# Two-layer transformer kernel: the rotary part of the latent attention scores from rounded values and their rests

## What is computed

```python
q = (rmsnorm_2(cq, q_norm_g) @ w_uq).reshape(B, S, MLA_HEADS, MLA_NOPE + MLA_ROPE)
q = jnp.concatenate([q[..., :MLA_NOPE], rope(q[..., MLA_NOPE:], pos)], axis=-1)
kv = (rmsnorm_2(ckv, kv_norm_g) @ w_ukv).reshape(B, S, MLA_HEADS, MLA_NOPE + MLA_V)
k_nope, v = kv[..., :MLA_NOPE], kv[..., MLA_NOPE:]
k_rope = rope(k_rope[:, :, None, :], pos)
k = jnp.concatenate([k_nope, jnp.broadcast_to(k_rope, (B, S, MLA_HEADS, MLA_ROPE))], axis=-1)
o = causal_block_attention(q, k, v).reshape(B, S, MLA_WIDTH)
```

## Time and profile before

| what | value |
|---|---|
| median of 3 runs | 2571.06 us (2571.04 to 2572.24) |
| the profiled execution | 2571.18 us, span 2569.4 us |
| PE busy | 2552.9 us, 99% of the span |
| DVE busy | 1731.5 us, 67% |
| ACT busy | 1248.0 us, 49% |
| chain that ended last | PE 97%, DVE 2% |
| granted TensorE clock, mean | 0.999 |
| score products L749 in the latent layer | 128 records, two for each of 64 products |

### The profile page before, as it was taken

One profiled execution on the slowest core, in us unless ns is written; L12 is line 12 of the kernel. 1 busy time (PEld: TensorE's weight loads), 2 busy tenths in 40 slices (PEclk: granted clock), 3 DMA queues, 4 the chain that ended last, 5 costly groups with the idle time before them and its releaser, 6 DMA issues.

```text
span 2569.4 us, 31110 instructions
## 1 busy us (share of the span) xinstructions
PE 2552.9 (99%) x12573; PEld 2160.0 (84%) x12573; DVE 1731.5 (67%) x1842; ACT 1248.0 (49%) x1625; POOL 36.3 (1%) x88
## 2 busy tenths in 40 slices
PE   9999999999999999999999999999999999999998
PEld 7888888888888888888888788888888888788997
DVE  6656555456676676676677658777777877755765
ACT  6444444445754445445447654444444444644544
POOL 0000000000000000000000000000000000000000
PEclk9999999999999999999999999999999999999999
DMA  9455465556687767777776557777777786655343
GB/s 325 164 168 176 164 208 189 193 190 227 214 282 255 278 246 266 269 255 270 258 251 209 203 184 266 258 272 277 259 268 272 247 290 204 206 192 176 119 163 131
DMA packets 278896, 580.91 MB, mean 226 GB/s; under 512 B 16368, under 2 KB 57584, under 8 KB 265584
## 3 DMA queue, kind: packets, MB, share of 16 engines
q1 hardware_dynamic: 256800, 467.70, 54.2%
q10 hardware_dynamic: 21968, 111.42, 11.4%
HBM read 576.96 MB, written 2.11 MB: 225 GB/s over the span
## 4 chain that ended last, share of the span: by engine, by line
PE 97%; DVE 2%; ACT 0%; DMA 0%; issue 0%; POOL 0%; SPq 0%; DVEq 0%; POOLq 0%; ACTq 0%
PE panels L601 16%; PE panels L602 16%; PE panels L606 16%; PE panels L636 8%; PE spare L601 6%; PE spare L602 6%; PE spare L606 6%; PE spare L636 5%; PE panels L644 4%; PE spare L644 2%; PE panels L1158 2%; PE spare L708 2%; PE panels L620 1%; PE panels L626 1%; PE panels L621 1%; PE spare L749 1%
## 5 line engine op out<-in xcount | busy, mean ns | idle before, releaser
L1981 DVE TENSOR_TENSOR lo<-raw,hi 128x1024 fp32r<-128x1024 f32 x827 | 1004.1, 1219 | 656.6 <-ACT hi L1277 653.2
L1277 ACT ACTIVATE hi<-raw 128x1024 fp32r<-128x1024 f32 x827 | 870.7, 1057 | 1049.1 <-PE panels L606 558.0
L601 PE MATMUL panels<-hi,xT 128*128 128x512 f32 x1220 | 480.4, 394 | 1.6 <-ACT hi L1277 1.4
L602 PE MATMUL panels<-hi,xT 128*128 128x512 f32 x1220 | 475.2, 390 | 0.0
L606 PE MATMUL panels<-lo,xT 128*128 128x512 f32 x1220 | 326.4, 389 | 0.0
L601 PEld LDWEIGHTS panels<-hi,xT 128*128 128x128 f32 x1220 | 229.1, 188 | 48.8 <-issue 1.7
L606 PEld LDWEIGHTS panels<-lo,xT 128*128 128x128 f32 x1220 | 229.0, 188 | 48.0
L602 PEld LDWEIGHTS panels<-hi,xT 128*128 128x128 f32 x1220 | 229.2, 188 | 46.5
L636 PE MATMUL panels<-xT,hi 128*128 128x512 f32 x896 | 224.5, 392 | 0.0
L2099 DVE SCALAR_TENSOR_TENSOR work<-work 128x2048 f32<-128x2048 f32 x96 | 219.2, 2284 | 0.0
L601 PE MATMUL panels<-hi,yT_hi 128*128 128x512 f32 x508 | 197.9, 390 | 0.0
(11 more groups left out here) (365 smaller groups left out, 3139.0 us busy)
## 6 DMA issues: line engine op xcount, KB each, us to landing
work<-k_ada_w ACTq DMA_DIRECT2D x96, 1024.0 KB, 5.9
raw<-w_in SPq DMA_DIRECT2D x76, 1024.0 KB
raw<-w_up SPq DMA_DIRECT2D x64, 1024.0 KB
raw<-w_down SPq DMA_DIRECT2D x64, 1024.0 KB
raw<-ret_w_in SPq DMA_DIRECT2D x64, 1024.0 KB
raw<-ret_w_in SPq DMA_DIRECT2D x64, 512.0 KB
raw<-ret_w_out SPq DMA_DIRECT2D x32, 1024.0 KB
raw<-mla_w_in SPq DMA_DIRECT2D x24, 1024.0 KB
```

Source lines behind the costliest of these rows:

```text
L601: pe.matmul(o, x_hi[:, kt0 + j, ms], hi_at(k)[:, at], start=first and j == 0, stop=False)
L602: pe.matmul(o, x_lo[:, kt0 + j, ms], hi_at(k)[:, at], start=False, stop=False)
L1277: act.activation(hi_at(k)[:, 0:words], raw[:, slot, k % 2 * CHUNK:k % 2 * CHUNK + words], copy).then_inc(hi_ready, 1)
L1981: dve.tensor_tensor(lo_at(k)[:, 0:words], raw[:, k // 2 % RAW_SLOTS, k % 2 * CHUNK:k % 2 * CHUNK + words], hi_at(k)[:, 0:words].bitcast(F3 ...
```

## The change

The rotary part of the scores is no longer one plain float32 product but two float32r products.

- DVE adds up the rotated queries in place, in `rope_cos` (`q_rotated`).
- ACT, at the end of step 4, copies each head's 64 rows to `r_split[:, hh]` with rounding (two 64x256 copies, `r_hi_ready`).
- DVE, at step 1 of the next turn, writes the rest of each head to the other 64 rows of `r_split[:, hh]` (`q_rest`, two 64x256 subtractions, `r_ready`). So one stationary tile holds the rounded query over its rest.
- The key's rounded part stands in both halves of `kr_hi_lo[:, 0]`, its rest in both halves of `kr_hi_lo[:, 1]`. Both are made once: ACT has two copies in place of one, DVE has two subtractions in place of two memsets.
- PE (`pair_scores`) makes, for each head and query block, two float32r products of 256 columns and then the nope product as before. For the first query block the rotary products cover 256 columns where 128 are needed; the second block then overwrites the surplus.
- `r_split` and `kr_hi_lo` lie in `pT_hi` and `pT_lo`, which the latent layer had not used. `rT` had a buffer for each of two pairs, `r_split` has one.

```diff
-        rT, krT = carve(3072, 2, TOKENS), carve(3584, 2, TOKENS)
+        r_split, kr_hi_lo = pT_hi, pT_lo
...
+            def pair_scores(b, q, hh):
+
+                open_score(b)
+                for m in range(TILES):
+                    o, ms, at = score[b][:, m * P:m * P + TOKENS], slice(m * P, (m + 1) * P), hh * TOKENS
+                    for c in range(2):
+                        pe.matmul(o, r_split[:, hh, ms], kr_hi_lo[:, c, :], start=c == 0, stop=False, skip_group_check=True)
+                    n = (m + 1) * P
+                    done = pe.matmul(o[:, 0:n], nqT[:, q, at + m * P:at + (m + 1) * P], nkT[:, q, at:at + n], start=False, stop=True,
+                                     skip_group_check=True)
+                done.then_inc(scored[b], 1)
+                t.nth(scored[b])
...
-                        pe.wait_ge(roped, t.nth(roped))
+                        pe.wait_ge(r_ready, t.nth(r_ready))
                         for hh in range(2):
-                            at = slice(hh * TOKENS, (hh + 1) * TOKENS)
-                            scores_of(1 - hh, [(nqT[:, q, at], nkT[:, q, at]), (rT[:, q, :], krT[:, hh, :])])
+                            pair_scores(1 - hh, q, hh)
...
-                    act.activation(krT[MLA_ROPE:P, 1, :], krT[0:MLA_ROPE, 0, :], copy).then_inc(kr_ready, 1)
+                    for half_of in (slice(0, MLA_ROPE), slice(MLA_ROPE, P)):
+                        done = act.activation(kr_hi_lo[half_of, 0, :], rope_cos[0:MLA_ROPE, :], copy)
+                    done.then_inc(kr_hi_ready, 1)
...
+                    if p is not None:
+                        act.wait_ge(q_rotated, t.nth(q_rotated))
+                        for hh in range(2):
+                            rows_of = slice(hh * MLA_ROPE, (hh + 1) * MLA_ROPE)
+                            done = act.activation(r_split[rows_of, hh, :], rope_cos[rows_of, :], copy)
+                        done.then_inc(r_hi_ready, 1)
...
-                    dve.memset(krT[MLA_ROPE:P, 0, :], 0.0)
-                    dve.memset(krT[0:MLA_ROPE, 1, :], 0.0)
...
+                if s == 4:
+                    dve.wait_ge(kr_hi_ready, 1)
+                    for half_of in (slice(0, MLA_ROPE), slice(MLA_ROPE, P)):
+                        done = dve.tensor_tensor(kr_hi_lo[half_of, 1, :], rope_cos[0:MLA_ROPE, :], kr_hi_lo[0:MLA_ROPE, 0, :].bitcast(F32),
+                                                 ALU.subtract)
+                    done.then_inc(kr_ready, 1)
...
-                dve.tensor_tensor(rT[:, p, :], rope_cos, rope_sin, ALU.add).then_inc(roped, 1)
+                dve.tensor_tensor(rope_cos, rope_cos, rope_sin, ALU.add).then_inc(q_rotated, 1)
+
+            def q_rest():
+
+                dve.wait_ge(r_hi_ready, t.nth(r_hi_ready))
+                for hh in range(2):
+                    rows_of, to = (slice(i * MLA_ROPE, (i + 1) * MLA_ROPE) for i in (hh, 1 - hh))
+                    done = dve.tensor_tensor(r_split[to, hh, :], rope_cos[rows_of, :], r_split[rows_of, hh, :].bitcast(F32), ALU.subtract)
+                done.then_inc(r_ready, 1)
+                t.nth(r_ready)
...
+                if s == 1 and q is not None:
+                    q_rest()
...
+                    if q is not None:
+                        dve.wait_ge(r_ready, t.now(r_ready))
```

More of the change, by code:

```diff
@@ L288, in build @@
         summed, og_ready = sem("summed"), sem("og_ready")
-        kr_half, kr_rotated, kr_ready = sem("kr_half"), sem("kr_rotated"), sem("kr_ready")
+        kr_half, kr_rotated, kr_hi_ready, kr_ready = sem("kr_half"), sem("kr_rotated"), sem("kr_hi_ready"), sem("kr_ready")
+        q_rotated, r_hi_ready, r_ready = sem("q_rotated"), sem("r_hi_ready"), sem("r_ready")
         q_nope_ready, k_nope_ready = sem("q_nope_ready"), sem("k_nope_ready")
@@ L386, in build @@
         LATENT = per_round(8, (2, 2), (2, 4), (2, 2), 0, (
-            (summed, 2), (og_ready, 2), (roped, 2), (q_nope_ready, 2), (k_nope_ready, 2), (max_ready, 2), (pair_exps_ready, 2), (turn_hi, 2), (dve_step, 4)))
+            (summed, 2), (og_ready, 2), (r_ready, 2), (q_rotated, 2), (r_hi_ready, 2), (q_nope_ready, 2), (k_nope_ready, 2), (max_ready, 2), (pair_exps_ready, 2), (turn_hi, 2), (dve_step, 4)))
         def ada_at(slots, count=ADA_PER_32):
@@ L2833, in _ @@
                     dve.wait_ge(dve_step, t.nth(dve_step))
-                    dve.tensor_tensor(krT[0:MLA_ROPE, 0, :], rope_cos[0:MLA_ROPE, :], rope_sin[0:MLA_ROPE, :], ALU.add).then_inc(kr_rotated, 1)
+                    dve.tensor_tensor(rope_cos[0:MLA_ROPE, :], rope_cos[0:MLA_ROPE, :], rope_sin[0:MLA_ROPE, :], ALU.add).then_inc(kr_rotated, 1)
                 split_lo()
```

## The result

| | before | changed |
|---|---|---|
| median of 15 runs | 2571.39 us (2570.35 to 2572.24) | 2576.78 us (2576.18 to 2579.45) |
| ratio, 95% interval | | 1.0021 (1.0014 to 1.0028) |
| span of the profiled execution | 2569.4 us | 2575.0 us |
| distance of two turns in the loop | 15.10 us | 16.28 us |

The change costs 5.4 us. That is inside the range on record, with the sign that was forecast, and 1.9 us more than the +3.5 of the sum. The ratio lies just over the 0.2% that was set as the bound between "the same" and "slower", and its interval has that bound in it; the likelier of the two had been "the same".

The account below looks back on a forecast made before the run. The ring of DVE and ACT was to replace PE as the bound, at 14.54+0.70+0.77=16.01 us per turn; PE's lateness of 4.17 less 0.7 saved gave +3.5, 2574.6 us, range 2568.2 to 2577.6.

Parts of the forecast that it names:

- the sum: Forecast change of the end time against the kernel before, +3.5 us, in general 6x+a-6.05.
- the ring: Maxima on DVE, exponentials and key copy on ACT, v copy and turn's rest on DVE; no PE; 14.54 us growing to 16.01.
- PE's saving of 0.35 us per pair: New scores on PE were to take 2.27 us in place of 2.62, 2.8 us saved over eight pairs.
- The switches between the two kinds of product: On PE at the scores, changes between float32 and float32r: taken as nothing, at most 0.7 us per pair.
- a=0.70: Time that ACT's two new copies per turn add to the ring, in us; low end 0.58, 0.84 without overlap.
- b=0.77: Time that DVE's two new subtractions per turn add to the ring at step 1, in us; upper end 0.9.
- The ring's slack of 0.56: Time per turn that the ring waited for PE before the turn's last chunk rest: 1.70-1.14 us.
- The margin at step 3: Lateness PE can absorb at step 3, where it needs ACT's copies of the turned exponentials: 1.4 us.
- x: Extra time per turn in the ring from copies and subtractions together, a+b, forecast 1.47 us.
- The prediction's slower rival: Four 64x256 operations and three handshakes paid in full, a=0.9, b=0.9: +5.7 us, 2576.7 us; chance 20%.
- PE's idle time: PE was to wait at step 3 for ACT's copy, some 5.9 us over five turns, about 1.2 per turn.
- The clock: Rival: PE's granted clock falls from 1.00 during its new waits, giving 2585 us or more; chance 3%.

Follow-up runs that it names:

- the 128-row run: The changed kernel with ACT's copies and DVE's rests made on all 128 rows instead of 64, same number of operations: 2572.89 us, ratio 1.0007.

## Why the prediction was right, and where it was short

- **The bound moves from PE to the ring: right.** The turn is 16.28 us and not PE's 14.73; shown by leaving out either side.
- **PE's saving of 0.35 us per pair: right**, 2.62 to 2.27 us, and 2.9 us with nothing else in the way. The switches between the two kinds of product cost nothing that shows.
- **a=0.70: too small, 0.85.** The row that was taken for it had an overlap at its end that the new place has not. The upper end, 0.84, was the value.
- **b=0.77: too small, 1.01**, and over the 0.9 that stood as the upper end. The first rest was taken whole, but the overlap as kept at the entry and at the exit; both are lost.
- **The ring's slack of 0.56: 0.68.** The prediction looked for a wait before the last chunk rest alone. A second stood in the masks, whose two operations took 1.13 us where they take 1.01 now:

```profile
2417.11 1.13 DVE L2133 SCALAR_TENSOR_TENSOR work<-spare,mask 128x384 f32<-128x384 f32 x2
```

  The scores ended at 2414.86+2.79=2417.65, when the first mask (0.55 us) was all but done, and the second, which ends at 2418.24, can't have begun before about 2417.69: it waited for its score. The idle column of that turn did not show it.
- **The margin at step 3: right**, 1.3 for 1.4. The error in a should have taken 0.15 from it, to 1.25. Not forecast was that PE also waits at step 2, 0.33 us for v's copy: the prediction had 2.4 us of margin there, counted against the old times of the exponentials. PE, whose own turn is 14.73, arrives earlier within a turn of 16.28. The sum is not changed by it, as step 3 still waits, and longer (0.59 us).
- **The sum:** 6x+a-6.05 had the right factor. Six turns carry x, so that 0.39 us of error in x is worth 2.3 us, and a's 0.15; the larger slack gives 0.7 back. +3.5 becomes +5.3, measured +5.4. The prediction's slower rival, small operations paid in full (x=1.8, +5.7), was the case that came true. It had a chance of 20%, which was too little, and against it stood that "every pair of rows shows an overlap of about 0.1". That is wrong: the four `q_rotate` operations of the same turn show none (1.73 us for four of 0.43), and nor do the two copies of the earlier trace rows between each other (the second starts 0.39 us after the first, which takes 0.38).
- **The rule of the Trainium skill** (VectorE: DVE Perf Modes, "The TRN2 errata"), a fixed cost for each small operation, gave an estimated +4.7 with nothing overlapped (its figures, 0.40 and 0.424 us, come to 4.6 in that sum). The traces agree with the size, 0.42 us for each. That twice the rows cost no more is not from that rule; the 128-row run shows it.
- **PE's idle time:** 5.9 us were forecast over five turns and 4.3 shown. The lateness was larger, not smaller; 0.62 of the 1.55 us that PE loses in a turn stand inside its records, before and after each wait.
- **The clock** stayed at 1.00 in turns with up to 0.62 us of wait at a time.

## What to carry to other kernels

An engine that is busy in 79% of a turn can be part of a chain that takes up 96% of it (DVE here, and the ring of 14.42 us in a turn of 15.10). Before adding to it, follow its longest wait to what ends it: if that goes back to the engine itself, the wait is latency of a ring, and work put anywhere in the ring but in such a wait counts in full once the ring's slack is used up. The same operations cost next to nothing if they are issued just before the wait, which is a matter of a few lines.

Small operations are priced by their full length unless a row shows the same neighbours at the same start rows. An error in a term that is paid in each turn comes back times the number of turns.

## What the runs showed of the hardware that was not expected

A pair of 64x256 operations that start at rows 0 and 64 in turn took 0.85 us of ACT and 1.01 of DVE, where a pair of 128x256 ones took 0.62 and 0.67, and a pair of copies on rows 0 to 63 alone 0.61. The loss is 0.11 to 0.13 us at each change of the operands' start row between 0 and 64, on both engines, in the three arrangements that have such changes, with the one exception named above.
